# Moving two transposes, six early units and twelve gather steps around the gate-matrix stage of a fused encoder step

## The reference, cut to what matters

```python
def peer_tokens(xt, w_query, sub_keys_1, sub_keys_2, u_table, v_table):
    q = (xt @ w_query).reshape(n, PEER_HEADS, 2, PEER_QDIM // 2)
    s1, s2 = q[:, :, 0] @ sub_keys_1.T, q[:, :, 1] @ sub_keys_2.T
    v1, i1 = lax.top_k(s1, 16);  v2, i2 = lax.top_k(s2, 16)
    sc, ci = lax.top_k(all 256 sums v1 + v2, 16)
    experts = e1 * 128 + e2            # 8 heads x 16 picks of 16384 experts
    gate = jax.nn.softmax(sc, axis=-1)
    act = jax.nn.gelu(jnp.einsum('nhkd,nd->nhk', u_table[experts], xt))
    return jnp.einsum('nhk,nhkd->nd', gate * act, v_table[experts])
```

## Time and profile before

| | us |
|---|---|
| median of three runs | 4613.14 (4604.13 to 4615.31) |
| the profiled execution, its own time | 4607.62 |
| its span in the trace | 4605.5 |
| PE busy | 4312.9 (94%) |
| DVE busy | 2690.1 (58%) |
| POOL busy | 2604.3 (57%) |
| ACT busy | 1045.4 (23%) |
| start of the gate-matrix stage on DVE, in the span | 2235.2 |
| last matmul of the gate-matrix stage starts | 2474.5 |
| first matmul of the late stage | 2489.5 |

### The profile page before, as it was taken

The page is one execution under the profiler, slowest core; times in us unless marked ns, Lnnn a source line. Parts: engine busy times, 40 slices in busy tenths (PEclk is TensorE's granted clock), DMA queues, the critical chain, the costliest instruction groups (busy, mean ns, idle before and its releaser), DMA issues.

```text
span 4605.5 us, 71897 instructions
## 1 busy us (share of the span) xinstructions
PE 4312.9 (94%) x26508; PEld 4131.9 (90%) x26508; DVE 2690.1 (58%) x4808; ACT 1045.4 (23%) x1845; POOL 2604.3 (57%) x1677
## 2 busy tenths in 40 slices
PE   8999999999989998999887999999999999999996
PEld 8999888888889997899777999999999999999996
DVE  1000233334432313899697777787777777787776
ACT  1000122222221101110223222222222322222323
POOL 4445332232235453347434777777777787777873
PEclk9999999999999999999999999999999999999998
DMA  5222322222233321113457999999999999999994
GB/s 199 101 98 98 119 104 109 100 92 74 78 135 120 102 100 66 55 64 115 151 161 233 392 390 387 386 394 385 408 389 384 398 409 411 392 407 413 410 411 186
DMA packets 269704, 1085.30 MB, mean 236 GB/s; under 512 B 24625, under 2 KB 91313, under 8 KB 185393
## 3 DMA queue, kind: packets, MB, share of 16 engines
q0 software_dynamic: 74736, 544.24, 28.9%
q1 hardware_dynamic: 86688, 388.01, 22.6%
q10 hardware_dynamic: 108192, 152.11, 9.8%
HBM read 1021.22 MB, written 68.42 MB: 237 GB/s over the span
## 4 chain that ended last, share of the span: by engine, by line
PE 51%; POOL 15%; DVE 12%; issue 10%; DMA 10%; ACT 1%; ACTq 1%; DVEq 0%; POOLq 0%
PE banks L463 29%; POOL w_lo L358 10%; PE banks L705 8%; PE banks L641 5%; DMA work<-in_v_rows,idx_all 4%; POOL work L386 4%; DMA work<-in_u_rows,idx_all 3%; PE banks L693 2%; PE banks L532 2%; PE banks L494 2%; POOL rows_own L386 1%; DVE banks L1425 1%; PE banks L502 1%; DVE work L1314 1%; DMA work<-out_p 1%
## 5 line engine op out<-in xcount | busy, mean ns | idle before, releaser
L358 POOL TENSOR_TENSOR w_lo<-w_raw,w_hi 128x1024 fp32r<-128x1024 f32 x464 | 1115.6, 2405 | 367.6 <-ACT w_hi L1026 362.3
L364 POOL TENSOR_SCALAR w_hi<-w_raw 128x2048 fp32r<-128x2048 f32 x138 | 267.5, 1939 | 1435.6 <-PE banks L463 1264.7
L463 PE MATMUL banks<-mv_hi,w_hi 128*128 128x256 f32 x3648 | 863.2, 318 | 63.3 <-DVE mv_lo L1148 37.9
L463 PE MATMUL banks<-mv_lo,w_hi 128*128 128x256 f32 x3648 | 836.1, 310 | 0.0
L463 PE MATMUL banks<-mv_hi,w_lo 128*128 128x256 f32 x3648 | 835.0, 310 | 0.0
L705 PE MATMUL banks<-mv_hi,w_hi 128*128 128x384 f32 x2048 | 702.0, 343 | 101.4 <-DVE work L1445 80.1
L463 PEld LDWEIGHTS banks<-mv_hi,w_hi 128*128 128x128 f32 x3648 | 651.7, 189 | 127.3 <-issue 102.8
L368 POOL TENSOR_TENSOR w_lo<-w_raw,w_hi 128x512 fp32r<-128x512 f32 x552 | 725.4, 1345 | 11.5
L641 PE MATMUL banks<-mv_hi,w_hi 128*128 128x384 f32 x2048 | 695.0, 339 | 18.1 <-POOL w_lo L358 13.9
L1026 ACT ACTIVATE w_hi<-w_raw 128x1024 fp32r<-128x1024 f32 x464 | 491.3, 1060 | 955.1 <-PE banks L705 788.2
L705 PE MATMUL banks<-mv_lo,w_hi 128*128 128x384 f32 x2048 | 694.1, 339 | 0.0
(11 more groups left out here) (162 smaller groups left out, 4784.8 us busy)
## 6 DMA issues: line engine op xcount, KB each, us to landing
w_raw<-in_wstream SPq DMA_DIRECT2D x464, 512.0 KB, 8.0
w_raw<-in_wstream SPq DMA_DIRECT2D x138, 1024.0 KB, 4.8
gate_matrix<-work ACTq DMA_DIRECT2D x12, 2048.0 KB, 9.2
work<-gate_matrix ACTq DMA_DIRECT2D x32, 768.0 KB, 9.5
out_p<-work ACTq DMA_DIRECT2D x34, 320.0 KB, 2.2
work<-out_p ACTq DMA_DIRECT2D x34, 320.0 KB, 3.5
gate_scratch<-work ACTq DMA_DIRECT2D x32, 320.0 KB, 2.2
work<-gate_scratch ACTq DMA_DIRECT2D x16, 640.0 KB, 4.0
```

The costliest lines, as they stand in the source:

```text
L358: pool.tensor_tensor(w_lo[s][:, part], raw[s][:, part], w_hi[s][:, part].bitcast(f32), ALU.subtract) \
L364: pool.tensor_scalar(w_hi[s][:, :], raw[s][:, :], 1.0, 0.0, ALU.mult, ALU.add).then_inc(hi_done, 1)
L463: last = pe.matmul(acc(dst, h), a[s][:, P * k:P * k + P], b[h][:, k, :], start=(k == k_first and n == 0), stop=(k == k_last and n == 2))
```

## The change

The two `natural` calls move ahead of the early units: `natural(1)` before unit 0 and `natural(0)` after unit 2. Six units instead of twelve are done ahead of the gate-matrix stage (`TAIL`), and the 96 groups take three k each instead of two (`GATE_UNITS`), so that they carry 18 units. The transposed picks go to banks 2, 3 and 1, and block B is copied out by way of `hb_t`. DVE does twelve of the gather steps (`FIRST`) inside the gate-matrix stage, one after every eighth group, on three row buffers; POOL fetches their rows between its splits. The loops of DVE, ACT and POOL in this stage are written out, so that the token's column of the picks is a fixed address instead of one from a register. ACT applies the activation of an early unit in the group that completes it, ahead of the store of the gate block. `deal()` deals the other steps over the same late units.

```diff
-TAIL = 12
-TAIL_PICKS = 10
+TAIL = 6
...
+FIRST = 12
+GATE_UNITS = 3
+GATE_Q = N2 // 4
...
+def place(n):
+    return n % (ROWS - 1) if n < FIRST else n % ROWS
 def arrivals(n):
-    return n // ROWS + 1 - (n % ROWS == ROWS - 1 and n > STEP_NORM)
+    if n < FIRST:
+        return n // (ROWS - 1) + 1
+    before = FIRST // (ROWS - 1) if place(n) < ROWS - 1 else 0
+    return before + (n - FIRST) // ROWS + 1 - (place(n) == ROWS - 1 and n > STEP_NORM)
...
+        hb_t = W2[:, 2 * N2:2 * N2 + D]
...
-        oh2 = m1_hi[:, 2 * EG * N2:2 * EG * N2 + 8 * P].rearrange("p (n e) -> p n e", n=8)
+        oh2 = m1_hi[:, 0:8 * P].rearrange("p (n e) -> p n e", n=8)
...
+        PICK_BANKS = (2, 3, 1)
...
-                pool.wait_ge(rows_used, n + 1)
+                pool.wait_ge(rows_used, n + 2 if n < FIRST + ROWS - 1 else n + 1)
                 pool.sem_inc(pool_apart, 1)
-                pool.indirect_dma_start(rows_t[n % ROWS], None, (u_rows, v_rows)[pick // PICKS % 2],
+                pool.indirect_dma_start(rows_t[place(n)], None, (u_rows, v_rows)[pick // PICKS % 2],
                                         bass.IndirectOffsetOnAxis(ap=idx_all[:, pick:pick + 1], axis=0)) \
-                    .then_inc(rows_in[n % ROWS], 16)
+                    .then_inc(rows_in[place(n)], 16)
...
-            with pool.Fori((U_PEER + TAIL) // 2 + 1, U_LATE // 2) as i:
-                for s in range(2):
-                    split_next(s, i)
+            fetched, late = ROWS - 1, N_EARLY - TAIL - 2
+            for j in range(late):
+                unit = U_PEER + TAIL + 2 + j
+                split_next(unit % 2, unit // 2)
+                upto = ROWS - 1 + FIRST * (j + 1) // (late + 2)
+                for n in range(fetched, upto):
+                    gather(n)
+                fetched = upto
             for s in range(2):
                 for h in range(2):
                     low(s, 0, h)
+                upto = ROWS - 1 + FIRST * (late + s + 1) // (late + 2)
+                for n in range(fetched, upto):
+                    gather(n)
+                fetched = upto
             for w in range(2):
                 pool.wait_ge(g_stored[w], 16 + 16 * (GBLK // 2))
-            gather(ROWS - 1)
+            gather(FIRST + ROWS - 1)
...
-            tail_units(0, TAIL_PICKS)
+            natural(1)
+            tail_units(0, TAIL // 2)
+            pe.wait_ge(hb_taken, 1)
+            natural(0)
+            tail_units(TAIL // 2, TAIL)
             pe.wait_ge(picks_done, 1)
             for q, src in enumerate((pick_g, pick_e[0], pick_e[1])):
+                if q == 2:
+                    pe.wait_ge(gelu_done, TAIL)
                 for b in range(N2 // P):
-                    last = pe.transpose(banks[:, 4 + q, P * b:P * b + P], src[:, 2 + b, :], ident)
+                    last = pe.transpose(banks[:, PICK_BANKS[q], P * b:P * b + P], src[:, 2 + b, :], ident)
                 last.then_inc(picks_full, 1)
             pe.wait_ge(picks_taken, 3)
-            natural(1)
-            tail_units(TAIL_PICKS, TAIL)
-            pe.wait_ge(hb_taken, 1)
-            natural(0)
             pe.sem_inc(g_full, 2)
-            with pe.Fori(0, GBLK // 2) as i:
-                for q in range(2 * GT // 4):
-                    for k in (2 * q, 2 * q + 1):
-                        s, n = k // KT_N, TAIL + 2 * i + k // KT_N
+            with pe.Fori(0, GATE_Q // 32) as i:
+                for q in range(32):
+                    for k in range(GATE_UNITS * q, GATE_UNITS * q + GATE_UNITS):
+                        s, n = k // KT_N % 2, TAIL + 2 * GATE_UNITS * i + k // KT_N
                         if k % KT_N == 0:
                             pe.wait_ge(split_done, U_PEER + n + 1)
                             pe.wait_ge(gelu_done, n - 1)
                         act_step(s, k % KT_N, s)
-                    pe.wait_ge(oh_ready, 16 * i + q + 1)
-                    pe.wait_ge(g_evac, 16 * i + q + 1)
+                    pe.wait_ge(oh_ready, 32 * i + q + 1)
+                    pe.wait_ge(g_evac, 32 * i + q + 1)
                     for t in range(4):
-                        n = 4 * (q % 2) + t
-                        last = pe.matmul(banks[:, 2 + q % 2, P * t:P * t + P], oh2[:, n, :].bitcast(f32), oh1[:, n, :],
-                                         start=True, stop=True)
+                        last = pe.matmul(banks[:, 2 + q % 2, P * t:P * t + P], oh2[:, 4 * (q % 2) + t, :].bitcast(f32),
+                                         oh1[:, 4 * (q % 2) + t, :], start=True, stop=True)
                     last.then_inc(g_full, 1)
...
-            for n in range(TAIL_PICKS - 2):
+            act.wait_ge(nat_ready, 1)
+            act.activation(hb_t, nat, ACT.Copy).then_inc(hb_taken, 1)
+            act.wait_ge(hb_taken, 1)
+            act.dma_start(hb_s, hb_t).then_inc(hb_stored, 16)
+            for n in range(TAIL - 2):
                 early_activation(n, n % 2, n // 2)
             act.wait_ge(gexp_in, 1)
             flat = pick_g.rearrange("p b k -> p (b k)")
             act.activation(flat, flat, ACT.Exp).then_inc(gexp_done, 1)
-            for n in range(TAIL_PICKS - 2, TAIL_PICKS):
+            for n in range(TAIL - 2, TAIL):
                 early_activation(n, n % 2, n // 2)
+            act.wait_ge(hb_stored, 16)
             for q in range(3):
                 act.wait_ge(picks_full, q + 1)
-                act.activation(pick_t[q], banks[:, 4 + q, 0:N2], ACT.Copy).then_inc(picks_taken, 1)
-            act.wait_ge(nat_ready, 1)
-            act.activation(rows_own[:, :], nat, ACT.Copy).then_inc(hb_taken, 1)
-            act.wait_ge(hb_taken, 1)
-            act.dma_start(hb_s, rows_own[:, :]).then_inc(hb_stored, 16)
-            for n in range(TAIL_PICKS, TAIL):
-                early_activation(n, n % 2, n // 2)
+                act.activation(pick_t[q], banks[:, PICK_BANKS[q], 0:N2], ACT.Copy).then_inc(picks_taken, 1)
+            act.wait_ge(picks_taken, 3)
             act.sem_inc(g_evac, 2)
-            with act.Fori(0, GBLK // 2) as i:
-                for q in range(2 * GT // 4):
-                    w, qq = q // 8, q % 8
-                    act.wait_ge(g_full, 16 * i + q + 3)
-                    if qq == 0:
-                        act.wait_ge(g_stored[w], 16 + 16 * i)
-                    act.activation(g_buf[w][:, :, 4 * qq:4 * qq + 4],
-                                   banks[:, 2 + q % 2, :].rearrange("p (t e) -> p e t", t=4), ACT.Copy).then_inc(g_evac, 1)
-                    if qq == 7:
-                        act.wait_ge(g_evac, 16 * i + q + 3)
-                        act.dma_start(G_s[:, :, ds(2 * i + w, 1), :, :].rearrange("g p a e t -> p g (a e t)"),
-                                      g_buf[w].rearrange("p (g e) t -> p g (e t)", e=EG)).then_inc(g_stored[w], 16)
-                    if q in (8, 15):
-                        early_activation(TAIL + 2 * i + q // 15, q // 15, TAIL // 2 + i)
+            early = TAIL
+            for q in range(GATE_Q):
+                blk, w, qq = q // 8, q // 8 % 2, q % 8
+                act.wait_ge(g_full, q + 3)
+                if qq == 0:
+                    act.wait_ge(g_stored[w], 16 + 16 * (blk // 2))
+                act.activation(g_buf[w][:, :, 4 * qq:4 * qq + 4],
+                               banks[:, 2 + q % 2, :].rearrange("p (t e) -> p e t", t=4), ACT.Copy).then_inc(g_evac, 1)
+                if GATE_UNITS * (q + 1) >= KT_N * (early - TAIL + 1):
+                    early_activation(early, early % 2, early // 2)
+                    early += 1
+                if qq == 7:
+                    act.wait_ge(g_evac, q + 3)
+                    act.dma_start(G_s[:, :, blk, :, :].rearrange("g p e t -> p g (e t)"),
+                                  g_buf[w].rearrange("p (g e) t -> p g (e t)", e=EG)).then_inc(g_stored[w], 16)
+            assert early == N_EARLY
...
             dve.wait_ge(picks_taken, 3)
...
-            dve.wait_ge(hb_stored, 16)
+            dve.sem_inc(rows_used, ROWS)
             dve.wait_ge(nat_ready, 2)
-            dve.sem_inc(rows_used, ROWS)
-            with dve.Fori(0, GBLK // 2) as i:
-                for q in range(2 * GT // 4):
-                    dve.wait_ge(g_full, 16 * i + q + 1)
-                    for t in range(4):
-                        n = 4 * (q % 2) + t
-                        tok = ds(2 * GT * i + 4 * q + t, 1)
-                        dve.tensor_scalar(oh2[:, n, :], iota, pick_t[2][:, tok], None, ALU.is_equal)
-                        last = dve.tensor_scalar(oh1[:, n, :], iota, pick_t[1][:, tok], pick_t[0][:, tok],
-                                                 ALU.is_equal, ALU.mult)
-                    last.then_inc(oh_ready, 1)
-            dve.wait_ge(g_full, 2 + N2 // 4)
-            dve.wait_ge(nat_ready, 2)
-            dve.sem_inc(out_evac, 4)
-            dve.sem_inc(w_ready, 2)
             def gather_step(n):
-                rows = rows_t[n % ROWS]
+                rows = rows_t[place(n)]
```

(17 more changed lines are left out.)

## The result

The changed kernel takes 4650.6 us (median of 4 runs, 4645.0 to 4653.6), beside 4614.2 us for the kernel before on the same chip: ratio 1.0081, 95% interval 1.0062 to 1.0100. It is slower by 0.8%. The forecast was 4630 us with a range up to 4646: right in its sign, 20 us too low, and the range ended 5 us too early. The profiled execution took 4644.98 us, its span is 4643.2.

What follows compares the result with a forecast made beforehand. PE was taken to bound the late stage and DVE the gate-matrix stage; 4607.6 - 43 (start) + 72 (gate-matrix stage) - 7 (late stage) gave 4630 us, with 8 in 10 for 4590 to 4646.

Steps and rivals of the forecast that it cites:

- the gate-matrix stage: Length from first one-hot row to last product: 312 us against 240.3, so 72 us lost, with DVE the bound.
- The start: Ahead of the gate-matrix stage: first one-hot row at 2192.1 instead of 2235.2, 43 us gained, both `natural` calls hidden.
- DVE's work in the stage: Gate-matrix stage: 174 us for 96 groups, 92 for 16 splits, 28 for twelve gather steps, together 294 us.
- The standing and the clock: Gate-matrix stage: 14 us for standing and other waits, 4 us for PE starting at its lower clock.
- rival (c): Gate-matrix stage: PE's clock falls more; three dips cost 7 us, with more standing 15; end 4645; chance 0.12.
- The steps: Gate-matrix stage: twelve gather steps of 2.35 us each add 28 us to DVE's work.
- The late stage: After the gate-matrix stage: 504 gather steps instead of 516 shorten PE's pauses, 7 us gained.
- Rival (b): Late stage: gathers pace it, twelve fewer gain 48 us, end 4589, or 4605 at DMA bandwidth; chance 0.15 for both.
- (a): Gate-matrix stage: fixed addresses shorten one-hot rows to about 0.13 us; stage 285 us, end 4603; chance 0.18.
- (d): Gate-matrix stage: twelve gather steps fall wholly inside splits, hiding 1.9 us each, 23 in all; end 4607; chance 0.08.

Runs made afterwards that it cites:

- unlocked rows: The changed kernel with one-hot rows reading the index row from PSUM (4570.8 us), or 129 elements long from a 3 x 43 source (4573.5 us).
- the steps apart from the splits: The changed kernel with gather steps behind groups 6 and 11 of every 16, in place of 7 and 15: 4643.6 us.

## Why the prediction was right in sign and wrong in size

The profiles differ by 37.6 us where the sum had -43 + 72 - 7 = 22. The miss of 16 us is that of the gate-matrix stage (87.3 in place of 72); that the start won 4 us more than forecast and the late stage 4 less is luck, the two cancel. The other 5 us of the 21 are the profiled execution, which lies 5.6 us below its kernel's median.

**The start.** Forecast 43 us, measured 47.2. The place of the picks and of both `natural` calls was read rightly. Five kernels with this same start code had their first row between 2187.0 and 2193.3, so the difference is what one profile varies by.

**DVE's work in the stage.** Forecast 174 + 92 + 28 = 294 us, measured 297.4: the rows and the steps as said, a split 5.95 us each ((297.4 - 174 - 28.2) / 16) in place of 5.74. Sixteen splits, as counted, with five slow rows each and not six. That DVE sets the stage with these terms was right, and the runs with room for four groups and with unlocked rows show it from both sides.

**The standing and the clock: the step that failed.** I took 14 us for the standing ("Walking the first 32 groups gives some 2 us of such standing in 16 groups") and 4 for the clock at the start, 18 together. DVE stood 29.9 us, some 5 in 16 groups. The timeline tells two kinds of this standing apart. The first, on DVE and then on PE:

```profile
2254.46 0.29 DVE L1440 TENSOR_SCALAR mv_hi<-cst,work 128x128 fp32r<-128x128 f32 x1 [0.55 <-PE banks L716]
2256.91 0.29 DVE L1440 TENSOR_SCALAR mv_hi<-cst,work 128x128 fp32r<-128x128 f32 x1 [0.56 <-PE banks L716]
```

```profile
2253.36 1.05 PE L716 MATMUL banks<-work,mv_hi 128*128 128x128 f32 x8
2255.82 1.05 PE L716 MATMUL banks<-work,mv_hi 128*128 128x128 f32 x8
```

PE is at full clock, a group every 2.45 us, and DVE, its lead of two groups full, stands 0.55 us in each. 23 of its 38 waits are of this kind, 12.8 us. The other 15, 16.0 us, are up to 2.0 us long, and each comes one or two groups behind a group that PE did at its lower clock: there DVE, whose split is over, catches up faster and fills its lead sooner. PE had fourteen such groups behind eight pauses, of 3.4 to 4.1 us; with the one at the start they cost it 16 us where I had 4, and 2.73 us in place of 2.45 for each of 32 groups behind a wait cost it 9 more. With its 235 us, 65.5 of waits for DVE and 1.0 for ACT that is its side of the 327.6.

How much of the standing would there be at full clock? This is an estimate, from a walk through all 96 groups with this profile's lengths (rows 0.20 and 0.26 us apart, one row through per instruction of POOL in splits of 7.1 us, steps of 2.2, PE 2.45 a group and 2.73 behind a wait). With the slow groups where the trace has them it gives 31 us of standing and a stage of 324; with none, 21 and 314. With room for four it gives stages of 286 and 273 us (measured 286.6 and 275.1); for the kernel without steps it has 49 us of standing where 41.9 were measured, so it is good to some 7 us. So both terms were too small: the walk, 21 in place of 14, and the clock, some 9 in place of 4. The clock was my rival (c), with three dips where there were eight; 4645 and a chance of 0.12 were too low.

That the two groups of room make the standing is shown: with four, at the same clock of 0.93, DVE did not stand, and the stage was 41 us shorter. How the standing divides between the splits and the clock is not shown by a run, since none holds the clock up while rows are shut out.

**The steps.** Forecast 28 us in the stage and 7 back, so 21; measured 7.4 between the medians with and without them. The rule that each step adds its length failed: of 28 us, 13 filled time in which DVE would have stood (41.9 against 28.8). That is luck for the forecast: without steps the same sum gives 284 us of stage, and 314.3 were measured, so the miss would have been 30 us and not 16.

**The late stage.** Forecast 7 us less, measured 2.6. In all twelve kernels it takes 2113 to 2124 us, with 504 or 516 steps, and the runs with 516 lie among the others, so the term is below what one profile can tell. Rival (b), gathers that pace it, needed 38 us and is out.

**The other rivals.** (a), short rows by fixed addresses, is refuted by the 0.20 and 0.25 us apart in the timeline. The Trainium skill, page VectorE: DVE Perf Modes, section on the TRN2 errata, has a fixed cost and the elements over the mode's factor, which by an estimate for these rows is 127 ns; the trace does not agree for rows with a column as scalar that follow each other. (d), steps hidden in splits, did not happen in this order of the groups, but the steps apart from the splits and the ring of four show its mechanism, worth 19 and 12 us of DVE's time beside the same kernels without steps.

## What to carry to other kernels

Where two engines feed each other through a short ring and one of them is stopped in bursts, don't add up the late engine's work alone: ask how much lead the ring holds against one burst, and walk the whole stage, first with PE at full clock and then with slower groups behind each pause. Doubling the ring was worth 39 us here, a little more than the whole change cost, some of it because steps then ran inside splits. And when many short DVE instructions stretch while POOL works, look first for a shape or a source that doesn't let POOL shut them out: it was worth 77 us for one element more.

## What the runs showed of the hardware

- A 128-element fp32 one-hot row, source and result in SBUF, starts 0.20 or 0.25 us before the next and is held up by each of POOL's instructions (1.30 us beside one of 1.2, 2.01 beside one of 1.92). With 129 elements in a 3 x 43 source and flat result it starts 0.25 or 0.31 us before the next, with its source in PSUM 0.26 or 0.32, and neither is ever held up (0.41 and 0.43 us at most). POOL's split takes 6.9 to 7.3 us where it holds rows up and 7.0 where it does not.
- A gather step of 2048 elements with one operand in PSUM takes 2.28 us inside a split and outside one.
- In the kernel without steps PE's clock fell to the lower level behind each of eleven pauses of 2.7 to 3.0 us and behind four of five pairs of 0.8 and 2.3 us, while behind the pairs of 1.8 and 2.65 us of the kernel before it fell in two of ten. What decides between them stays open.
